# A memory normalised one stage earlier, and two sets of PSUM reads moved from DVE to ACT

## The reference, cut to what matters

```python
def second_block(x, mem, ...):
    h = x                                     # the first block's output
    mem_n = rmsnorm(mem, norm_mem_w)          # mem * rsqrt(mean(mem^2) + eps) * weight
    h = h + head_group_mixer(rmsnorm(h, norm_mix_w), ...)
    h = h + memory_cross_attention(rmsnorm(h, norm_xattn_w), mem_n, xq_w, xkv_w, xo_w)
    h = h + sq_relu_mlp(rmsnorm(h, norm_mlp_w), mlp_up_w, mlp_down_w)
    return rmsnorm(h, norm_f_w)

def memory_cross_attention(h, mem_n, xq_w, xkv_w, xo_w):
    q = h @ xq_w                              # 4 heads of 256
    k, v = split(mem_n @ xkv_w)
    p = softmax(q @ k.T * 256 ** -0.5)
    return (p @ v) @ xo_w
```

## Time and profile before

| | |
|---|---|
| median of 3 runs | 1014.54 us (1014.43 to 1014.72) |
| profiled execution: its time, its span | 1016.42 us, 1014.6 us |
| PE busy | 988.9 us, 97% |
| DVE busy | 697.7 us, 69% |
| ACT busy | 507.6 us, 50% |
| mean granted TensorE clock | 0.994 |
| DMA | 172.82 MB, mean 170 GB/s |

### The profile page before, as it was taken

How to read it: one execution, slowest core, us unless ns; L and a number is a source line. 1 busy time by engine, 2 the same in 40 slices (tenths; PEclk the granted TensorE clock), 3 DMA queues, 4 the chain that set the end, 5 groups by cost and what they waited for, 6 DMA issues and landing times.

```text
span 1014.6 us, 19909 instructions
## 1 busy us (share of the span) xinstructions
PE 988.9 (97%) x7365; PEld 932.3 (92%) x7365; DVE 697.7 (69%) x1267; ACT 507.6 (50%) x820; POOL 37.6 (4%) x53
## 2 busy tenths in 40 slices
PE   9999999999999999999999999899999999999996
PEld 8999999998988898999998899787899899998885
DVE  5766665554687769766675659988875488885553
ACT  6544444463465666645454456332664365454441
POOL 4500000010010000000000000000000000000000
PEclk9999999999999999999999999999999999999999
DMA  7554465437543345555566464312543355555551
GB/s 255 190 181 167 177 231 177 140 111 263 207 152 113 108 146 187 187 186 186 186 209 216 159 247 167 123 64 104 207 159 135 106 180 198 189 192 194 172 198 45
DMA packets 46028, 172.82 MB, mean 170 GB/s; under 512 B 5434, under 2 KB 6226, under 8 KB 45456
## 3 DMA queue, kind: packets, MB, share of 16 engines
q1 hardware_dynamic: 44352, 163.20, 46.3%
q0 software_dynamic: 1472, 8.76, 2.6%
q10 hardware_dynamic: 144, 0.03, 0.0%
HBM read 170.90 MB, written 3.77 MB: 172 GB/s over the span
## 4 chain that ended last, share of the span: by engine, by line
PE 79%; DVE 12%; ACT 3%; DMA 3%; issue 3%; SPq 0%; DVEq 0%; ACTq 0%
PE bank L401 18%; PE bank L402 18%; PE bank L403 18%; PE bank L405 12%; PE bank L406 6%; DVE cy L1491 3%; DVE wlo L379 3%; DMA raw<-in_w_mix 2%; ACT whi L368 1%; PE bank L1285 1%; DVE x L490 1%; DVE res L715 1%; PE bank L1677 1%; PE bank L1654 1%; PE bank L892 1%
## 5 line engine op out<-in xcount | busy, mean ns | idle before, releaser
L401 PE MATMUL bank<-x,whi 128*128 128x256 f32 (+1 forms) x1464 | 421.9, 288 | 2.6 <-DVE x L490 1.6
L402 PE MATMUL bank<-x,whi 128*128 128x256 f32 (+1 forms) x1464 | 415.7, 284 | 0.0
L403 PE MATMUL bank<-x,wlo 128*128 128x256 f32 (+1 forms) x1464 | 415.2, 284 | 0.0
L379 DVE TENSOR_TENSOR wlo<-raw,whi 128x1024 fp32r<-128x1024 f32 (+1 forms) x285 | 359.6, 1265 | 21.5 <-ACT whi L368 21.4
L368 ACT ACTIVATE whi<-raw 128x1024 fp32r<-128x1024 f32 (+1 forms) x285 | 309.0, 1087 | 112.1 <-PE bank L403 62.0
L401 PEld LDWEIGHTS bank<-x,whi 128*128 128x128 f32 x1464 | 277.5, 190 | 11.2 <-issue 4.6
L403 PEld LDWEIGHTS bank<-x,wlo 128*128 128x128 f32 x1464 | 277.4, 190 | 0.0
L402 PEld LDWEIGHTS bank<-x,whi 128*128 128x128 f32 x1464 | 276.8, 189 | 0.2
L405 PE MATMUL bank<-hid,whi 128*128 128x512 f32 x432 | 151.9, 395 | 0.0
L406 PE MATMUL bank<-hid,wlo 128*128 128x256 f32 x432 | 121.5, 281 | 0.0
L405 PEld LDWEIGHTS bank<-hid,whi 128*128 128x128 f32 x432 | 81.2, 188 | 19.3
(11 more groups left out here) (277 smaller groups left out, 1188.6 us busy)
## 6 DMA issues: line engine op xcount, KB each, us to landing
raw<-in_w_f2in SPq DMA_DIRECT2D x44, 512.0 KB, 3.4
raw<-in_w_f1in SPq DMA_DIRECT2D x42, 512.0 KB, 3.5
raw<-in_w_mix SPq DMA_DIRECT2D x35, 512.0 KB, 3.9
raw<-in_w_up SPq DMA_DIRECT2D x32, 512.0 KB, 4.2
raw<-in_w_down SPq DMA_DIRECT2D x32, 512.0 KB, 4.2
raw<-in_w_f1out SPq DMA_DIRECT2D x16, 704.0 KB, 4.1
raw<-in_w_f2out SPq DMA_DIRECT2D x16, 704.0 KB, 4.2
raw<-in_w_mixb SPq DMA_DIRECT2D x20, 512.0 KB, 3.5
```

The lines of the kernel that those rows point to most:

```text
L379: nc.vector.tensor_tensor(wlo[:, s, 0:tiles * P], raw[:, s, 0:tiles * P], whi[:, s, 0:tiles * P], ALU.subtract).then_inc(w_lo, 1)
L401: nc.tensor.matmul(out, whi[:, s, w], hi, start=first, stop=False)
L402: nc.tensor.matmul(out, whi[:, s, w], lo, start=False, stop=False)
L403: mm = nc.tensor.matmul(out, wlo[:, s, w], hi, start=False, stop=last)
```

## The change

The memory is loaded after the first strip of `f2in`. Ahead of its part in `f2out` ACT squares the whole memory in two operations and scales its eight tiles; DVE adds the squares up in three operations; TensorE makes one group of token sums instead of eight (after the second strip of `f2out`) and spreads the reciprocal (after the fourth). In the last body ACT copies the spread to `memr` and DVE multiplies the memory itself by it, in two operations. The 16 key and value tiles then need no factor: ACT copies them out of PSUM, in place of DVE's multiplications. To have the memory in SBUF earlier, its tile is placed past the part of the area that the FFN uses, with `km` and `cy` ahead of it.

The diff, cut to its core:

```diff
+        def act_memory(act):                      # ahead of act_residual("f2out")
+            act.wait_ge(mem_in, 16)
+            for a in (0, HALF):
+                nc.scalar.activation(msq8[:, a:a + HALF, :], mem[:, a:a + HALF, :], ACT.Square).then_inc(m_sq, 1)
+            act.wait_ge(m_sq, 2)
+            for e in range(KT):
+                nc.scalar.activation(mem[:, e, :], mem[:, e, :], ACT.Copy, scale=gain(N_MEM, e)).then_inc(m_scaled, 1)
+        def dve_memory(dve):                      # ahead of dve_residual("f2out")
+            dve.wait_ge(m_sq, 2)
+            for n in (4, 2, 1):
+                if n < 4:
+                    dve.wait_ge(m_added, 2 // n)
+                nc.vector.tensor_tensor(msq8[:, 0:n, :], msq8[:, 0:n, :], msq8[:, n:2 * n, :],
+                                        ALU.add).then_inc(m_added, 1)
+        def pe_memory(pe, i, j):
+            if (i, j) == (0, 1):
+                pe.wait_ge(m_added, 3)
+                token_sums(ps[5], msq8[:, 0, :], blocks(NX), one_col, True, True).then_inc(m_stat, 1)
+            if (i, j) == (0, 3):
+                pe.wait_ge(m_inv, 1)
+                spread(ps[7], col_inv[:, 0, :], blocks(NX)).then_inc(m_bc, 1)
+        def act_memory_norm(act, i, j):
+            if (i, j) == (0, 2):
+                act.wait_ge(m_stat, 1)
+                nc.scalar.activation(col_root[:, 0, 0:2], ps[5][:, 0:2], ACT.Sqrt, ...).then_inc(m_sd, 1)
+            if (i, j) == (3, 0):
+                act.wait_ge(m_bc, 1)
+                nc.scalar.activation(memr[:, :], ps[7][:, 0:NX], ACT.Copy).then_inc(m_r, 1)
+        def dve_memory_norm(dve, i, j):
+            if (i, j) == (0, 2):
+                dve.wait_ge(m_sd, 1)
+                nc.vector.reciprocal(col_inv[:, 0, 0:2], col_root[:, 0, 0:2]).then_inc(m_inv, 1)
+            if i == 3 and j in (0, 1):
+                if j == 0:
+                    dve.wait_ge(m_r, 1)
+                    dve.wait_ge(m_scaled, KT)
+                own = mem[:, HALF * j:HALF * (j + 1), :]
+                nc.vector.tensor_tensor(own, own, memr[:, :].unsqueeze(1).to_broadcast([P, HALF, NX]),
+                                        ALU.mult).then_inc(m_normed, 1)
...
 def pe_mixb(pe):
                     if q == 20:
-                        pe.wait_ge(m_scaled, KT)
+                        pe.wait_ge(m_normed, 2)
-                if MEM0 < q <= MEM0 + KT:
-                    e = q - MEM0 - 1
-                    pe.wait_ge(m_sq, e + 1)
-                    token_sums(ps[5], msq[:, e % 2, :], blocks(NX), one_col, e == 0, e == KT - 1).then_inc(m_stat, 1)
-                if q == 15:
-                    pe.wait_ge(m_inv, 1)
-                    pe.wait_ge(rot_step, 12)
-                    spread(ps[7], col_inv[:, 0, :], blocks(NX)).then_inc(m_bc, 1)
...
 def act_mixb(act):     # after split_hi of the step, ahead of everything else in it
+                if q >= 20:
+                    act.wait_ge(pe_done, sc + q + 1)
+                    act.wait_ge(acc_free, sgrp + q)
+                    nc.scalar.activation(km[:, q - 20, :], ps[banks[sgrp + q]][:, 0:NX], ACT.Copy).then_inc(acc_free, 1)
-                if MEM0 <= q < MEM0 + KT:      # square and scale of one tile a step
...
-                if q == MEM0 + KT + 1:         # root
...
-                if q == 15:                    # memr
...
 def dve_mixb(dve):
-                dve_mixb_read(dve, q)
+                if q < 20:
+                    dve_mixb_read(dve, q)
-                if q == 14:
-                    dve.wait_ge(m_sd, 1)
-                    nc.vector.reciprocal(col_inv[:, 0, 0:2], col_root[:, 0, 0:2]).then_inc(m_inv, 1)
...
 def dve_mixb_read(dve, q):
-                if q == 20:
-                    dve.wait_ge(m_r, 1)
-                nc.vector.tensor_tensor(km[:, q - 20, :], out, memr[:, :], ALU.mult).then_inc(acc_free, 1)
...
 def act_xattn(act):    # between the exponentials and the copy out of bank 3
+                if KT <= m < XSTEPS:
+                    e = m - KT
+                    act.wait_ge(pe_done, qc + m + 1)
+                    act.wait_ge(acc_free, qg + m)
+                    if e >= 2:
+                        act.wait_ge(xv_tr, e - 1)
+                    dst = tu if e % 2 else tg
+                    nc.scalar.activation(dst[:, 0:NX], ps[banks[qg + m]][:, 0:NX], ACT.Copy).then_inc(acc_free, 1)
                 if KT + 2 <= m < XSTEPS + 2:
                     e = m - 2 - KT
                     act.wait_ge(xv_tr, e + 1)
...
 def dve_xattn(dve):
-                        nc.vector.tensor_tensor(dst[:, 0:NX], out, memr[:, :], ALU.mult).then_inc(acc_free, 1)
...
 POOL
+            pool.wait_ge(pe_done, first["f2in"][0] + 1)
+            pool.dma_start(mem[:, :, :], io["mem"]).then_inc(mem_in, 16)
             pool.wait_ge(pe_done, sc)
             nc.gpsimd.memset(glu[:, :, 0:TAPS - 1], 0.0).then_inc(glu_zero, 1)
-            pool.dma_start(mem[:, :, :], io["mem"]).then_inc(mem_in, 16)
+            pool.wait_ge(m_stat, 1)
             pool.dma_start(decay[:, :, :], io["decay"]).then_inc(decay_in, 16)
```

More of the change, by code:

```diff
@@ L208, in build @@
         mem2 = place("mem2", [P, KT, 2, NX], F32R, at)
+        km = place("km", [P, KT, NX], F32, at)
+        cy = place("cy", [P, 4, NX], F32, at)
+        assert at[0] >= area + 2 * FT * NX * 4
         mem = place("mem", [P, KT, NX], F32, at)
-        km = place("km", [P, KT, NX], F32, at)
         glu_at = at[0]
         glu = place("glu", [P, 4, TAPS - 1 + NX], F32, at)
-        cy = place("cy", [P, 4, NX], F32, at)
         qr = place("qr", [P, 4, NX], F32, at)
@@ L233, in build @@
         vmem = place("vmem", [P, 2, D], F32, at)
+        at = [decay_at]
+        msq8 = place("msq8", [P, KT, NX], F32, at)
         at = [decay_at]
@@ L639, in build, with pe_residual @@
         halves = {"wo": 0, "f2out": KT, "wo2": 2 * KT, "xo": 3 * KT, "down": 4 * KT}
-        def pe_residual(pe, name, cpm, width, rhs, ready, late=0):
+        def pe_residual(pe, name, cpm, width, rhs, ready, late=0, extra=None):
             c0, g0 = first[name]
@@ L674, in body, with act_residual @@
                     one(out, j, before=wait).then_inc(pe_done, 1)
+                    if extra is not None and edge:
+                        extra(pe, i, j)
             bodies(pe, counts[name], per, body)
-        def act_residual(act, name, n, full, cpm, prep=True):
+        def act_residual(act, name, n, full, cpm, prep=True, extra=None):
             c0, g0 = first[name]
@@ L692, in body, with dve_residual @@
                                                  scale=gain(n, k)).then_inc(og_set, 1)
+                    if extra is not None and edge:
+                        extra(act, i, j)
             bodies(act, counts[name], per, body)
-        def dve_residual(dve, name, n, full, cpm, scale, prep=True):
+        def dve_residual(dve, name, n, full, cpm, scale, prep=True, extra=None):
             c0, g0 = first[name]
@@ L707, in body @@
                         dve.wait_ge(pe_done, c0 + per * i + j + 1)
+                        if name in ("wo2", "xo") and edge and k == 0:
+                            dve.wait_ge(acc_free, g0)
                         if full:
@@ L726, in body @@
                         dve_square(dve, n, k, full, m % 2)
+                    if extra is not None and edge:
+                        extra(dve, i, j)
             bodies(dve, counts[name], per, body)
@@ L1258, in build @@
         RET0 = 13
-        MEM0 = 4
         LN0 = 24
@@ L1304, in pe_mixb @@
                     pe.wait_ge(acc_free, sgrp + 8 + e + 1)
+                    if e == 1:
+                        pe.wait_ge(m_r, 1)
                     if e >= 2:
@@ L1394, in pe_retention @@
                 token_sums(ps[3], msq[:, t % 2, :], blocks(NX), head_cols, True, True).then_inc(gn_var, 1)
+        def act_memory(act):
[22 more added lines that the diff above has]
+                act.wait_ge(m_stat, 1)
+                nc.scalar.activation(col_root[:, 0, 0:2], ps[5][:, 0:2], ACT.Sqrt, bias=epsc[:, 0:1],
+                                     scale=1.0 / D).then_inc(m_sd, 1)
+            if (i, j) == (3, 0):
[12 more added lines that the diff above has]
+                                        ALU.mult).then_inc(m_normed, 1)
         def act_mixb(act):
@@ L1405, in act_mixb @@
                     nc.scalar.activation(cosv[:, :], angle[:, :], ACT.Sin, scale=0.5).then_inc(cs_act, 1)
-                if MEM0 <= q < MEM0 + KT:
-                    e = q - MEM0
-                    if e == 0:
-                        act.wait_ge(mem_in, 16)
-                    if e >= 2:
-                        act.wait_ge(m_stat, e - 1)
-                    nc.scalar.activation(msq[:, e % 2, :], mem[:, e, :], ACT.Square).then_inc(m_sq, 1)
-                    act.wait_ge(m_sq, e + 1)
-                    nc.scalar.activation(mem[:, e, :], mem[:, e, :], ACT.Copy, scale=gain(N_MEM, e)).then_inc(m_scaled, 1)
+                if q >= 20:
```

(12 more changed lines are left out.)

16 lines of the change are left out of this document (3 added, 13 removed).

## The result

The changed kernel takes 1025.15 us (median of 9 runs, 1019.65 to 1028.13) beside 1014.72 for the kernel before (9 runs in the same session): a ratio of 1.0089, interval 1.0073 to 1.0105. On the 1014.54 from which the forecast started that ratio makes 1023.6, 9.0 more; the forecast was 6.3 more. The ratio puts it inside the range of 1017.6 to 1024.5; the runs' own median lies 0.65 above it. A second set of 6 runs gave 1023.93, ratio 1.0077 (1.0054 to 1.01). The profiled execution has a span of 1021.3, 6.7 longer than that of before, and a time of 1023.51, 7.1 longer.

What follows compares the result with a forecast made beforehand. TensorE was taken as the bound, busy 988.9 of 1014.6 us, with DVE setting the pace in the projections. The terms 0.7 - 0.7 + 6.3 = +6.3 on the median 1014.54 gave 1020.8 us, range 1017.6 to 1024.5.

Steps and rivals of the forecast that it cites:

- The values, +6.3: Cross attention, steps 10 to 15: TensorE waits for two ACT copies in a row, 1.05 us a step, +6.3 us.
- The second FFN, +0.7: Second FFN's output: TensorE gets one group of token sums and one spread, +0.7 us, bounds 0.35 to 0.9.
- The projections: Second mixer's projections: nothing gained until 647 as DVE sets the pace, then -1.2 us from the removed statistic's wait.
- The keys: Memory keys: -2.2 us at 700, of which -0.7 is left after TensorE's waits caused by ACT's in-order queue.
- The rival that the hand-over is hidden: Attention steps 10 to 15: ACT's copies out of bank 3 are done in time, sum 0; chance 0.07.
- The backlog in the second FFN: ACT's backlog reaches TensorE, with table load or memory transfer late: up to 3 us more; chance 0.06.
- That all work taken from TensorE and DVE counts: Removed token sums, statistic's wait and DVE reads all shorten the kernel, to 1007.7 us; chance 0.03.
- The rival of the clock in the new gaps: TensorE's clock falls in the six value gaps or at the rotation, one to three times: 1022.5 to 1026; chance 0.22.

Runs made afterwards that it cites:

- early_load: The kernel before with the change's places for `mem`, `km` and `cy` and its early load, normalisation still in the mixer: 1015.5 us, ratio 1.0002.
- v_order: The changed kernel with ACT's copy out of bank 3 ahead of its copy of the value strip: 1016.36 us, ratio 1.0001.
- v_only: The kernel before with only the values' copies on ACT in the changed order, values left unmultiplied by the memory's factor: 1022.11 us, ratio 1.0054.
- norm_only: The changed kernel with key and value strips copied by DVE as plain copies, leaving the early load and normalisation: 1015.32 us, ratio 1.0004.
- both_late: `v_order` with each key copy also put at the end of its step in ACT's queue: 1014.04 us, ratio 0.9983.
- k_dve: The changed kernel with the key strips copied by DVE (plain copy), the values as changed: 1022.04 us, ratio 1.0071.
- a_again: The changed kernel, unchanged, run again on the chip of the next three experiments: 1023.93 us, ratio 1.0077.
- v_fill: The changed kernel with three small matmuls of constants ahead of each TensorE wait for `xv_copied`: 1021.99 us, ratio 1.0054.
- pe_spread: The kernel before with two small transpositions of a constant on TensorE behind the fourth strip of the second FFN's output: 1019.19 us, one run.

## Why the prediction was right, and where its terms were off

The sign, the mechanism and the order of size held. With `early_load` as the mixer without a stretch at half clock, the stages of the changed kernel sum to +1.4 in the FFN, -0.1 in the mixer, +5.9 in the attention: +7.2. The two ratios, times 1014.54, give 9.0 (7.4 to 10.7) and 7.8 (5.5 to 10.1). Two of the three terms were 0.6 to 0.7 too low and the largest 0.4 too high, so part of the agreement is luck: the sum of 6.3 is 0.9 under what the stages show. The range of 1017.6 to 1024.5 holds by the ratio; the runs' own median of 1025.15 is outside it, and what fills the 1.9 between the stages' sum and the first ratio is in part open (below).

- **The values, +6.3: measured +5.87**, 0.98 a step of which 0.84 is idle. It is one order in one queue, shown from both sides: `v_order` takes all of it away, `v_only` brings all of it alone. Of the four parts of the step of 1.05 the last three (two copies and the way to TensorE, 0.80) are as put: 776.49 to 777.29. The first was 0.26; in the changed kernel ACT starts 0.19 after TensorE could have (the strip's last matmul starts at 776.18, and before the change the transposition followed such a matmul by 0.12).
- **The second FFN, +0.7: measured +1.42**, twice the term and outside its bounds of 0.35 to 0.9. The step that failed is "whatever is put into its queue there is paid in full", read as: and nothing else is. The groups themselves cost what was put: in `norm_only` the sums move the strips behind them by 0.45 and the spread by 0.22, 0.67 in all. What the term lacked is the 0.0044 us by which the distance of every one of the 176 pairs of matmuls is longer in the changed kernel, 0.77 in all (0.58 in `norm_only`, where it begins behind the spread). The cover of ACT and DVE held, with the table load and the first late weight copy where the working put them.
- **The projections: nothing until 647 held to 0.02**: from the FFN's token sums to the transposition of `tu` it is 49.39 before and 49.41 after, with the first rotation's wait at the 2.7 foretold. Of the -1.2 behind it, 0.75 came. The first keys strip starts 75.28 us after those token sums before, 73.55 in the changed kernel, but 74.30 in `early_load`: -1.73 in the pair of profiles, -0.75 at the same clock. The 1.22 of the earlier trace rows itself was read rightly, although it lies behind a stretch at half clock: in `early_load`, at full clock, it is 1.27.

```profile
651.43 0.43 PE L424 MATMUL bank<-ident,col_inv 128*128 128x128 f32 x2 [0.33 <-DVE col_inv L1517]
...
652.70 0.41 PE L1317 MATMUL bank<-ident,tg 128*128 128x128 f32 x2 [0.84 <-ACT v L1429]
```

  The step that failed is "DVE follows, as it was TensorE that it waited for by then". The turning of `tg` did come 1.35 earlier (55.32 us after the token sums in `early_load`, 53.97 in `norm_only`), but right behind it TensorE waits 0.49 for DVE's `amat`, which is as late as before: the next thing that TensorE waits for took the rest.
- **The keys: -0.7 left for the whole mixer. The pair of profiles shows -1.11; at the same clock it is -0.13.** The terms behind the first keys strip held. The table load behind the first copy was to take back 0.35: the taps start 6.68 us behind the first keys strip, 6.34 in `norm_only`. The four reads taken from DVE were to bring 1.36: from those taps to `ones` times `cy` it is 20.68, 21.98 in `norm_only`, so they brought 1.30. From there to `wo2` ACT's order was to cost 1.5; it cost 1.58, by the two hand-overs foreseen: the squares 1.2 (measured 1.08), the root 0.2 (0.24). So most of what the sum lacks (0.45 of 0.57) is what DVE's `amat` kept. `both_late`, which keeps the gains without the hand-overs, is 2.9 shorter in the mixer than `early_load`, and `k_dve` shows that the keys' move as made is a loss of 0.62.
- **The rival that the hand-over is hidden** fell: the wait is 0.84, far over its limit of 0.33. **The backlog in the second FFN** never reached TensorE. **That all work taken from TensorE and DVE counts** fell too: before 647 nothing was gained, and the free values cost 5.87.
- **The rival of the clock in the new gaps** failed as it was put. In the profiles of the changed kernel, `a_again`, `k_dve` and `v_only`, all with the six gaps, the clock is 1.00 through all of the attention, and `v_only` costs 5.5 us with a clock like that of before. The clock did fall in the other place that the rival named, behind the rotation's 2.7 (first two rows: the changed kernel; third: `norm_only`, with the same wait of 2.71 and no fall):

```profile
624.00:632.00 8.00, 5.28 (x30) 4.97 (x30) 7.90 (x17) 1.06 (x1) 0.00 (x0) 0.79 0.46 166
648.00:656.00 8.00, 6.55 (x52) 5.45 (x53) 7.97 (x17) 1.81 (x4) 0.00 (x0) 1.00 0.35 123
...
624.00:632.00 8.00, 5.31 (x40) 5.08 (x41) 8.00 (x18) 2.12 (x2) 0.00 (x0) 1.00 0.38 132
```

  It costs nothing there, as DVE sets the pace until 647. The fall behind the wait of 1.29 in the earlier trace rows does not come each time either: `early_load` waits 1.30 at that place and keeps its clock. The price of 1.7 for a stretch is right where nothing covers it (1.69 in `v_fill`); at the place it was read from it is 0.98.
- **Open**: the runs of the changed kernel are spread over 8.5 us and their times go with their clocks (1019.65 at 0.995, 1028.13 at 0.989); their mean clock is 0.992 (0.9928 in `a_again`) beside 0.9948 for before. `v_order` (0.9926) and `k_dve` (0.9923) share this, `norm_only` (0.9937) and `both_late` (0.9938) in part, `v_only` and `early_load` (0.9951) don't. So some runs have more stretches at half clock than their profile does, and they come with the early normalisation rather than with the values; this is a correlation over 5 to 12 runs each, and in which stage they fall was not seen. It may be most of the 1.9 us by which the first ratio exceeds the stages' sum; its interval reaches down to 0.2 from that sum. Another 0.3 lies outside the span: the time of a run is 2.13 above its span in the changed kernel (mean of nine) and 1.87 in the kernel before.

## What to carry to other kernels

In a queue that runs in order, an instruction that waits for the newest thing holds up everything behind it until that thing is done: before work is moved to an idle engine, write down its queue for one step, and put what frees a buffer for the bound engine ahead of what waits for that engine. Here this order was worth 5.9 us, and 2.73 in the mixer for the key copies, while the move itself was worth nothing for the values (58.44 in `v_order` and in `norm_only`) and about 1.7 for the keys (`both_late` against `norm_only`: 2.13 less in the mixer, 0.47 more in `wo2`). When a wait is taken away, look for what the engine will wait for next: behind the removed 1.2 us stood DVE's `amat`, and 0.75 was left. And compare stages only between executions with the clock at the same level there: the pair of profiles showed 1.0 us of gain in the mixer that was the clock's.

## What the runs showed of the chip that was not expected

- **The distance between large matmuls has two values, and a few small ones can switch it for the rest of a stage**: 0.3489 us or 0.3533 for a pair of 512 and 256 columns, for up to 64 us, at a granted clock of 1.00 in both. Two small matmuls brought the longer one, four set it back in `k_dve` and `v_fill`. `wo2` has the longer in the kernel before too, and the shorter in `k_dve` and `v_fill` from its second strip on, which makes that stage 0.2 shorter. What decides was not found. The Trainium skill (TensorE: Matmul & The Clock Gate, Back-to-back issue gap) gives N / 2.4 + 2.5 ns for an isolated matmul; an estimate from it for such a pair is 0.325, and neither measured value agrees.
- **No drain behind a table load is seen**: 1.30 us from the load's start to that of the square root. The Trainium skill (ScalarE: Activation LUTs, What ACT_TABLE_LOAD costs) has another 1.38 for a drain; by it, as an estimate, the root would start at 549.0; the trace has it at 547.67.
- **The stages of two executions agree to 0.02 us while the kernel's time varies by 8**: where the difference is sought in a stage, one profile settled more than ten timed runs. The profiles differ elsewhere: the start of the second FFN's output lies between 531.92 us (`v_fill`) and 534.62 (`pe_spread`), and all but `v_fill` and `k_dve` have one or two stretches at half clock between 240 and 294, far ahead of the change.
